# Issuing both halves of a page pair from SyncE in a two-layer decoder step

## What is computed

```python
pool = cache_nsa_kv[l]                      # (n_pool, 128, 4, 2, 64): k_cmp, v_cmp, k_sel, v_sel
past = pool[page_table].reshape((dec_b, past_len) + pool.shape[2:])
...
chunks = kv_full[:, :n_chunk * CMP_STRIDE, :2]         # k_cmp, v_cmp: 16 positions to a chunk
hid = jax.nn.gelu(chunks[:, :-1] @ w1h[:, 0] + chunks[:, 1:] @ w1h[:, 1] + pe_term)
cmp = hid @ w2                                         # compressed keys and values
...
ls = einsum(qh, k_sel of the selected blocks) + bias   # scores of the selected branch
```

## Time and profile before

| what | value |
|---|---|
| median of 3 runs | 1672.32 us (1670.66 to 1675.72) |
| the profiled execution: device time | 1674.17 us |
| the profiled execution: span of the instructions | 1672.5 us |
| PE busy | 1546.5 us |
| ACT busy, DVE busy, POOL busy | 338.7, 356.7, 156.7 us |
| mean granted TensorE clock | 0.964 |
| table reads with page halves, SP and POOL | 64 each |

### The profile page before, as it was taken

The page is one execution under the profiler, slowest core; times in us unless marked ns, Lnnn a source line. Parts: engine busy times, 40 slices in busy tenths (PEclk is TensorE's granted clock), DMA queues, the critical chain, the costliest instruction groups (busy, mean ns, idle before and its releaser), DMA issues.

```text
span 1672.5 us, 22848 instructions
## 1 busy us (share of the span) xinstructions
PE 1546.5 (92%) x8232; PEld 1145.9 (69%) x8232; DVE 356.7 (21%) x1056; ACT 338.7 (20%) x880; POOL 156.7 (9%) x256
## 2 busy tenths in 40 slices
PE   8879999998799899999989989999879998999996
PEld 5537577766477677777755647777656776777774
DVE  1223335442011211100023232443300112110001
ACT  1132422223211111100023252222321102110002
POOL 1123420000000100000202424000000010000000
PEclk9889999998899999999999999999889999999998
DMA  9772667445455366556836454853535544665561
GB/s 259 187 193 71 169 210 239 138 140 164 137 172 195 101 202 199 177 182 243 249 114 168 119 151 116 289 167 124 161 93 203 194 151 139 211 205 186 187 215 63
DMA packets 212258, 287.85 MB, mean 172 GB/s; under 512 B 13781, under 2 KB 201383, under 8 KB 210888
## 3 DMA queue, kind: packets, MB, share of 16 engines
q1 hardware_dynamic: 194262, 189.01, 37.8%
q10 hardware_dynamic: 7858, 72.49, 11.4%
q0 software_dynamic: 10048, 25.19, 5.7%
HBM read 276.74 MB, written 72.49 MB: 209 GB/s over the span
## 4 chain that ended last, share of the span: by engine, by line
PE 82%; DMA 7%; DVE 3%; ACT 3%; SPq 2%; issue 2%; POOLq 0%; ACTq 0%; POOL 0%; DVEq 0%
PE psum L1412 76%; PE psum L1416 6%; DMA pages<-in_cache_nsa_kv 3%; DMA toep_scratch<-arena 2%; DMA kv_ring<-in_cache_dil_w 1%; DMA block_no<-const_block_no 1%; SPq L496 1%; ACT regrouped L816 1%; SPq L561 1%; DVE arena L1385 0%; ACT logit L937 0%; ACT xT L1020 0%; POOLq L681 0%; DVE logit L1309 0%; SPq L449 0%
## 5 line engine op out<-in xcount | busy, mean ns | idle before, releaser
L1412 PE MATMUL psum<-arena,w_ring 128*128 128x288 f32 (+3 forms) x2816 | 681.7, 404 | 14.2 <-ACT arena L1020 9.3
L1412 PEld LDWEIGHTS psum<-arena,w_ring 128*128 128x128 f32 x2816 | 534.8, 191 | 156.5 <-issue 15.6
L1412 PE MATMUL psum<-xT,w_ring 128*128 128x288 f32 x1408 | 358.2, 411 | 0.0
L1412 PEld LDWEIGHTS psum<-xT,w_ring 128*128 128x128 f32 x1408 | 265.2, 191 | 79.9 <-issue 10.3
L1394 DVE TENSOR_TENSOR arena<-arena 128x288 f32 x64 | 29.3, 458 | 223.4 <-ACT arena L1030 223.4
L1013 ACT ACTIVATE arena<-arena 128x576 f32<-128x576 f32 x16 | 10.7, 683 | 323.9 <-DVE arena L1383 323.9
L757 POOL TENSOR_TENSOR arena<-arena 128x288 f32<-128x288 f32 x12 | 9.5, 792 | 675.2 <-DVE arena L1375 675.2
L1030 ACT ACTIVATE arena<-psum 128x288 f32<-128x288 f32 x64 | 26.2, 410 | 220.7 <-PE psum L1412 220.7
L1416 PE MATMUL psum<-ident,regrouped 128*128 128x128 f32 (+1 forms) x300 | 49.5, 287 | 20.1 <-DVE arena L1165 10.4
L1412 PE MATMUL psum<-arena 64*128 64x128 f32 (+6 forms) x276 | 63.1, 359 | 2.3 <-DVE arena L1071 2.2
L1416 PE MATMUL psum<-ident,logit 128*128 128x128 f32 (+1 forms) x272 | 47.1, 301 | 17.9 <-DVE logit L1356 9.0
(11 more groups left out here) (206 smaller groups left out, 1179.8 us busy)
## 6 DMA issues: line engine op xcount, KB each, us to landing
w_ring<-in_w_ff SPq DMA_DIRECT2D x64, 1024.0 KB, 5.7
w_ring<-in_w_in SPq DMA_DIRECT2D x44, 1024.0 KB, 7.4
out<-in_cache_dil_w ACTq DMA_DIRECT2D x8, 1984.0 KB
pages<-in_cache_nsa_kv POOLq DMA_DIRECT2D x64, 192.0 KB, 4.5
pages<-in_cache_nsa_kv SPq DMA_DIRECT2D x64, 192.0 KB, 4.5
kv_ring<-in_cache_dil_w SPq DMA_DIRECT2D x20, 512.0 KB, 4.9
w_ring<-in_w_o SPq DMA_DIRECT2D x8, 1024.0 KB, 6.2
out<-in_cache_nsa_win ACTq DMA_DIRECT2D x8, 992.0 KB
```

Source lines behind the costliest of these rows:

```text
L1412: return T.matmul(out, w, x, start=start, stop=stop, **kw)
```

## The change

SP's `load_tile` issues the second half too, directly behind the first, onto the semaphore that POOL used (`pg2_rdy`). POOL's `load_tile` and its three loops go. Nothing else is edited: the waits of PE and ACT, the slots, the sizes and the order of all other loads are as before. The line numbers behind the edit shift (POOL's `page` read is L683 in the changed kernel, the value load L689).

```diff
@@ SyncE, load_tile
                     b, m = t // 4, t % 4
                     sp.dma_start(pages[0:64, s], page(b, 2 * m)[:, :, 0:3].rearrange(
                         "o (q s) c h d -> (o q) s (c h d)", s=2)).then_inc(pg_rdy[s].sem, 16)
+                    sp.dma_start(pages[64:128, s], page(b, 2 * m + 1)[:, :, 0:3].rearrange(
+                        "o (q s) c h d -> (o q) s (c h d)", s=2)).then_inc(pg2_rdy[s].sem, 16)
@@ GpSimd
-                def load_tile(t):
-
-                    p = position(t)
-                    s = p % PG_SLOTS
-                    v = p - PG_SLOTS + 1
-                    pool.wait_ge(kst.sem, kst.after(l, max(v - (1 if v > P_TILE else 0), 0)))
-                    pool.sem_inc(pool_steps, 1)
-                    pool.wait_ge(rg.sem, rg.after(l, max(v, 0)))
-                    pool.sem_inc(pool_steps, 1)
-                    b, m = t // 4, t % 4
-                    pool.dma_start(pages[64:128, s], page(b, 2 * m + 1)[:, :, 0:3].rearrange(
-                        "o (q s) c h d -> (o q) s (c h d)", s=2)).then_inc(pg2_rdy[s].sem, 16)
@@ GpSimd, the order of a layer
-                for t in range(4):
-                    load_tile(t)
                 load_kv(1)
...
-                for t in range(4, 18):
-                    load_tile(t)
                 lend(0, 0)
                 lend(0, 1)
                 load_kv(2)
-                for t in range(18, 32):
-                    load_tile(t)
                 load_kv(4)
```

## The result

The changed kernel takes 1715.04 us (median of 4 runs, 1703.62 to 1717.32), the kernel before 1671.49 us in the same session (4 runs). The ratio is 1.0259, with a 95% interval of 1.0226 to 1.0292: slower by 2.6%. The profiled execution took 1715.08 us with a span of 1713.4 us, 40.9 us over the span before. In the page, PE's busy time rose by 20 us at a lower mean clock, POOL lost its 64 page halves, and SPq's share of the chain went from 2% to 5%.

What follows compares the result with a forecast made beforehand. TensorE was taken to bound the kernel as a whole, and transfers the tile stages, where SP would become the limit. Stages +44.0, start -1.5 and clock +3.0 gave +45.5 us on 1674.17, so 1718 us as median, range 1700 to 1735.

Steps and rivals of the forecast that it cites:

- SP's pace: Tile stages: SP issuing both halves needs 2.75 us per tile (1.44 + 1.31), against 1.65 us before.
- Rival 2: Tile stages: the second half costs its issue alone, 1.98 us per tile; 1683 us, or up to 1700; chance 9%.
- The four stages: Tile stages, two per layer: longer by 9.0, 10.9, 13.0 and 11.1 us, in sum +44.0 us.
- The landing: Tile stages: transfers fall to 143 GB/s, DMA share about 0.6, and a half lands in about 3.3 us.
- The start of layer 0: Up to the bias table's landing: -5.6 us from earlier constants, +4.1 from value loads; -1.5 taken, ends -5.6 and +3.2.
- Start of layer 1: SP has 5.2 us more to issue ahead of the first weights; charged 0, without cover 5 us.
- The clock: Lower PE clock at the ends of tile stages: one cost of +3 us in all, ends 0 and 11.
- Rival 3: Clock falls in all four tile stages, PE's time per tile doubling from 1.46 to 2.9 us: 1733 us; chance 13%.
- The sum: Whole kernel: 44.0 - 1.5 + 3.0 = +45.5 us on the profiled 1674.17; 1718 us as median.
- Rival 1: Tile stages: transfers stay the limit, at most 1.65 us per tile; 1667 us, faster 3%, about no change (1672) 3%.
- the rule: Tile loads: several issuing engines save only sequencer time, usually small against the DMA; the sum would be near 0.
- C: Theory from the experiments, not the prediction: tile stages share the 16 DMA engines with value loads now running beside the tiles.

Runs made afterwards that it cites:

- run with the start alone: The kernel before, with only the second halves of tiles 0 to 3 of each layer issued by SP: 1662.94 us, ratio 0.9977; repeated 1665.63 us, 0.9969.
- run with the busier PE: The changed kernel, with the key transposes of tiles 4 to 14 of each group done four times: 1713.82 us, ratio 1.0255.
- its control: The kernel before, with page numbers fixed at build time in the tile loads of both SP and POOL: 1666.0 us, ratio 0.9979.

## Why the prediction was right, point by point

- **SP's pace.** 2.75 us per tile was forecast, 1.44 + 1.31; it is 1.43 + 1.30 = 2.73. Rival 2, that the second half costs its issue alone, falls with it. It would have been right, at 0.64 us, only without the table read.
- **The four stages.** +9.0, +10.9, +13.0 and +11.1 (+44.0) were forecast; +7.7, +11.7, +15.0 and +12.8 (+47.2) came, in which the clock has its part of 3.8 us (below). Without it they are +7.3, +11.7, +12.3 and +12.1, together +43.4. That the sum is off by only 0.6 us is partly luck: the first stage was forecast 1.7 us too long, the others 0.8 too short, 0.7 too long and 1.0 too short. Once a stage ran, no tile waited for a slot.
- **The landing.** The step "a half should land in about 3.3 us" at a DMA share of 0.6 failed in three stages. It was 3.2 us in the first (92 to 121 us) but 5.2, 3.6 and 4.2 us (medians) in the others, with shares of 1.01, 0.66 and 0.92. I had placed the value loads beside the bias table alone; those of the second groups also run beside tiles, since POOL no longer has tiles ahead of them. This cost little, as the run with the value loads held back shows: each transfer lies behind SP's pace, and only that of the last tile counts.
- **The start of layer 0.** -1.5 was the value taken, -5.6 the end; -4.3 came. The write of the bias table began 4.8 us earlier and took 36.70 us instead of 36.24. The charge of 4.1 us for the value loads beside it was wrong: the write took 36.47 us in the run with the start alone, without them, so they cost it some 0.2 us, no more than such executions differ. From 74.8 us on POOL issues one only every 2 us while the write runs, as its timeline shows (the last bracket is idle time before); behind the write it is one every 1.16 us. So some 7 of them, 0.5 MB, ran beside the write, not the 0.95 MB taken. Why the issues are slower there stays open. The repeated run with the start alone shows the same gain by itself.

```profile
74.82 0.62 POOL L689 DMA_DIRECT2D w_ring<-in_cache_nsa_kv  x1 [20.74 <-issue]
76.92 0.60 POOL L689 DMA_DIRECT2D w_ring<-in_cache_nsa_kv  x1 [1.48 <-issue]
...
91.83 0.60 POOL L689 DMA_DIRECT2D w_ring<-in_cache_nsa_kv  x1 [0.56 <-issue]
92.97 0.60 POOL L689 DMA_DIRECT2D w_ring<-in_cache_nsa_kv  x1 [0.55 <-issue]
```

- **Start of layer 1.** Charged at 0. From the start of layer 0's second compression product to the first tile of layer 1 pass 695.6 us, where it was 698.8. Over the profiled executions of all runs this stretch lies between 694.9 and 703.4 us, whatever the edit, so no cost shows above that spread.
- **The clock.** +3 us were taken for one stage end at the lower level; the ends cost 3.8: in layer 1's first group the last tile before the prompt's starts at 947.24 with the clock down, and from there to the compression product pass 11.5 us against 8.9 before, +2.7; the second group has +0.7. The two ends of layer 0 have +0.4 and 0. The run with the busier PE gave back 2.1 and 1.4 us in just the two stages of layer 1. Rival 3 (all stages at PE's pace, 1733) falls: with the clock at 0.94 to 1.00 the stages keep their length. The rest of the program was 2.0 us shorter. The clock fell at other places there (0.90 for 391 to 426 us, where it was 0.80), which may be the reason; the spread named above is larger, so this part isn't shown to be the change's.
- **The sum.** 43.4 (stages) + 3.8 (clock at their ends) - 4.3 (start) - 2.0 (the rest) = +40.9 us, against 44.0 + 3.0 - 1.5 = +45.5. The sums of the stages and of the clock were off by less than 1 us each; the start was taken 2.8 us too dear, and the 2.0 us of the rest had no term.
- **Rival 1 and the rule.** The transfers are the limit again only where SP is rid of the reads, and the stages keep their length only if the value loads are held back too: the run with both has 0.9977, its control 0.9979. So the rule of the Trainium skill, page "DMA: Bandwidth & Descriptors", section "Issuing engines are not separate DMA queues", holds here for the transfers: one issuing engine filled the 16 DMA engines as two did. Its "usually small" for the issue does not hold where each one carries a table read: 2.73 us on SP for 1.65 us of transfer.

The second limit, C, was in no rival. It had no effect on the forecast, but a mending of the change that frees SP alone runs into it.

## What to carry to other kernels

Before issues are gathered on one engine, take one issue with all that belongs to it (register loads, address steps, waits) from start to start in the timeline, multiply by what a tile needs, and compare with the time of its transfer: here 2.73 against 1.65 us, and the excess times the exposed tiles was nearly all of the loss (1.08 x 45 = 49 us of stages estimated, 46 to 47 measured). Where an engine is emptied, look at what stands next in its queue; it comes earlier, and it shares the DMA engines with what you wanted to speed up. A part of a bad change can be good: the four tiles at the start were worth 0.3% alone.

## What was not expected of the hardware

- A register load of a table entry on SP takes 0.26 to 0.28 us and 0.15 us of address step, and 24 of them in a row went at one per 0.57 us (13.0 us between the first and the last of 24), without any overlap.
- One hardware queue reached 251 GB/s on these rows of 1536 bytes at a share of 1.01, no less than a hardware and a software queue together (241 at 1.05).
- Other loads beside the tiles reach back to the issuer by way of the slots: without reads but with value loads beside the tiles (share 1.08) a half took 8.3 us to land, and SP waited for slots; with the value loads held back it took 4.9 us (163 to 183 us, share 1.01). In the changed kernel with late values, at a share of 0.55, it took 3.0 us. Single issues on SP also grew now and then, from 0.54 to 1.41 us in the run without reads, but to 1.13 us in the one with late values as well (DMA share 0.61 and 0.57 around it), so full engines are not shown to be the reason.
- A PE that works little in the tiles got 0.80 of the clock, and one that repeats transposes 0.94 to 1.00, with the same time: in these stages, where PE waits for loads, the lower level cost time only at their end.
